# Experts' weights requested as one transfer per matrix in place of two halves

## The reference, cut to what matters

```
xb  = hf[toks]                                   # 128 rows at most, x 1024
hid = silu(xb @ w_g[e]) * (xb @ w_u[e])          # w_g, w_u: 1024 x 512
yb  = (hid @ w_d[e]) * wb[:, None]               # w_d: 512 x 1024
y   = zeros.at[row_tok].add(yb)
```

## Time and profile before

| | us |
|---|---|
| median of 3 runs | 2850.39 (2847.27 to 2853.35) |
| profiled execution, its own time | 2851.61 |
| span of the profiled execution | 2849.8 |
| ACT's first work on experts' weights | 2209.9 |
| second expert's first request | 2231.8 |
| last request of weights issued | 2802.2 |

### The profile page before, as it was taken

The page is one execution under the profiler, slowest core; times in us unless marked ns, Lnnn a source line. Parts: engine busy times, 40 slices in busy tenths (PEclk is TensorE's granted clock), DMA queues, the critical chain, the costliest instruction groups (busy, mean ns, idle before and its releaser), DMA issues.

```text
span 2849.8 us, 36330 instructions
## 1 busy us (share of the span) xinstructions
PE 2702.4 (95%) x13108; PEld 2215.8 (78%) x13118; DVE 1981.0 (70%) x2396; ACT 1467.3 (51%) x2248; POOL 523.4 (18%) x394
## 2 busy tenths in 40 slices
PE   7999999999989999999999989899999899999996
PEld 6787978878767667887888877787778788888875
DVE  6776756565655554565545888898764798989885
ACT  5544436443436665443333457534422577777774
POOL 0000500000117665001000000000010154334332
PEclk9999999999989999999999999999999899999998
DMA  5511057653885764761221100112132799999995
GB/s 173 206 52 59 17 166 279 237 206 109 288 251 128 165 165 126 258 225 37 100 71 48 46 15 1 45 45 82 67 113 111 277 380 376 370 362 367 361 362 171
DMA packets 197118, 492.83 MB, mean 173 GB/s; under 512 B 75089, under 2 KB 75217, under 8 KB 172400
## 3 DMA queue, kind: packets, MB, share of 16 engines
q1 hardware_dynamic: 173760, 448.83, 46.1%
q10 hardware_dynamic: 14000, 25.30, 2.5%
q0 software_dynamic: 9216, 16.81, 2.4%
HBM read 436.01 MB, written 71.63 MB: 178 GB/s over the span
## 4 chain that ended last, share of the span: by engine, by line
PE 53%; DMA 12%; DVE 8%; POOL 6%; issue 4%; ACT 3%; SPq 0%; POOLq 0%; DVEq 0%; ACTq 0%; PEldq 0%
DMA ex_raw<-in_w_up_e 7%; PE ps L1439 7%; PE ps L1442 6%; PE ps L1441 6%; POOL fa_pl L2035 6%; PE ps L921 5%; PE ps L922 5%; PE ps L923 5%; PE ps L3664 4%; DMA ex_raw<-in_w_down_e 3%; DVE ex_w L3814 3%; ACT ex_w L3749 2%; PE ps L3392 1%; PE ps L2767 1%; PE ps L2414 1%
## 5 line engine op out<-in xcount | busy, mean ns | idle before, releaser
L3814 DVE TENSOR_TENSOR ex_w<-ex_raw,ex_w 128x2048 fp32r<-128x2048 f32 x190 | 430.8, 2290 | 63.5 <-ACT ex_w L3749 61.3
L3749 ACT ACTIVATE ex_w<-ex_raw 128x2048 fp32r<-128x2048 f32 x190 | 361.7, 1916 | 107.0 <-DMA ex_raw<-in_w_up_e 59.2
L3664 PE MATMUL ps<-ex_w,ex_xT 128*128 128x512 f32 x1536 | 367.8, 395 | 12.8 <-DVE ex_xT L3829 12.8
L3664 PEld LDWEIGHTS ps<-ex_w,ex_xT 128*128 128x128 f32 x1536 | 287.2, 190 | 78.4 <-issue 13.1
L2035 POOL TENSOR_TENSOR fa_pl<-fa_p,fa_ph 128x512 fp32r<-128x512 f32 x192 | 196.3, 1040 | 108.2 <-ACT fa_ph L2137 104.1
L798 DVE SCALAR_TENSOR_TENSOR arena<-arena,small 128x1023 f32<-128x1023 f32 (+9 forms) x168 | 213.5, 1271 | 3.7
L1571 DVE TENSOR_TENSOR bs_b<-arena,bs_b 128x512 fp32r<-128x512 f32 x160 | 110.4, 690 | 139.4 <-ACT bs_b L1465 139.1
L1465 ACT ACTIVATE bs_b<-arena 128x512 fp32r<-128x512 f32 x160 | 100.1, 629 | 201.6 <-PE ps L1442 178.7
L3664 PE MATMUL ps<-ex_w,ex_hT 128*128 128x512 f32 x768 | 184.5, 396 | 0.7 <-issue 0.5
L3664 PEld LDWEIGHTS ps<-ex_w,ex_hT 128*128 128x128 f32 x768 | 143.0, 189 | 31.3 <-issue 1.9
L1850 DVE TENSOR_REDUCE small<-ps 128x1 f32<-128x512 f32 (+1 forms) x192 | 101.2, 554 | 84.5 <-PE ps L1829 45.4
(11 more groups left out here) (492 smaller groups left out, 6820.5 us busy)
## 6 DMA issues: line engine op xcount, KB each, us to landing
ex_raw<-in_w_gate_e SPq DMA_DIRECT2D x64, 1024.0 KB, 13.8
ex_raw<-in_w_up_e SPq DMA_DIRECT2D x64, 1024.0 KB, 13.6
ex_raw<-in_w_down_e SPq DMA_DIRECT2D x64, 1024.0 KB, 14.1
bs_a<-h_ops SPq DMA_DIRECT2D x100, 512.0 KB, 4.3
arena<-in_w_in SPq DMA_DIRECT2D x56, 512.0 KB, 3.7
zu_a<-h_ops SPq DMA_DIRECT2D x56, 512.0 KB, 3.9
arena<-in_w_in SPq DMA_DIRECT2D x26, 1024.0 KB, 6.5
h_ops<-ko_s SPq DMA_DIRECT2D x16, 512.0 KB, 6.2
```

The lines of the kernel that those rows point to most:

```text
L3664: mm = nc.tensor.matmul(out, l, r, start=(k == 0 and n == 0), stop=(k == kc - 1 and n == 2))
L3749: nc.scalar.activation(half_of(part[m][0], h), raw[m][:, h * W // 2: (h + 1) * W // 2], ACT.Identity).then_inc(high[m], 1)
L3814: V.tensor_tensor(half_of(part[m][1], h), raw[m][:, h * W // 2: (h + 1) * W // 2], half_of(as_f32(part[m][0]), h), ALU.subtract)\
```

## The change

The raw buffers stay as they are. A matrix is now one request of 2 MB with 16 KB per partition, with one semaphore; SP waits until DVE has made both low parts of the previous expert's matrix, and ACT waits for the whole matrix before it begins the first half. ACT's and DVE's instructions stay in halves, and so do PE's waits. The same is done for the last expert's DOWN and for the path that handles experts with more tokens than a place holds.

```
-def load_half(sp, raw, experts, e, loaded, m, h):
-    half = slice(h * KC * DE // 2, (h + 1) * KC * DE // 2)
+def load_whole(sp, raw, experts, e, loaded, m):
     of = experts[m][bass.ds(e, 1)].rearrange("a (p k) n -> p (a k n)", p=P)
-    sp.dma_start(raw[m][:, half], of[:, half]).then_inc(loaded[m][h], 16)
+    sp.dma_start(raw[m], of).then_inc(loaded[m], 16)
...
         def load(i, s, which):
             b = i * ns + s
             for m in which:
-                for h in range(2):
-                    sp.wait_ge(low[m], b * 2 + (h + 1))
-                    load_half(sp, raw, experts, b, loaded, m, h)
+                sp.wait_ge(low[m], b * 2 + 2)
+                load_whole(sp, raw, experts, b, loaded, m)
...
             if now is LAST:
-                for h in range(2):
-                    sp.wait_ge(low[GATE], 2 * NE + 2)
-                    load_half(sp, [raw[GATE]] * 3, experts, NE - 1, [last_loaded] * 3, DOWN, h)
+                sp.wait_ge(low[GATE], 2 * NE + 2)
+                load_whole(sp, [raw[GATE]] * 3, experts, NE - 1, [last_loaded] * 3, DOWN)
...
                 act.wait_ge(used[m], b + 1)
+                act.wait_ge(loaded[m], b * 16 + 16)
                 for h in range(2):
-                    act.wait_ge(loaded[m][h], b * 16 + 16)
                     nc.scalar.activation(half_of(part[m][0], h), raw[m][:, ...
```

More of the change, by code:

```diff
@@ L3467, in expert_raw @@
     return [c.named(f"ex_raw{m}", *((3, 0), (3, W), (5, W))[m], W) for m in range(3)]
-def load_half(sp, raw, experts, e, loaded, m, h):
-    half = slice(h * KC * DE // 2, (h + 1) * KC * DE // 2)
+def load_whole(sp, raw, experts, e, loaded, m):
     of = experts[m][bass.ds(e, 1)].rearrange("a (p k) n -> p (a k n)", p=P)
-    sp.dma_start(raw[m][:, half], of[:, half]).then_inc(loaded[m][h], 16)
+    sp.dma_start(raw[m], of).then_inc(loaded[m], 16)
 def load_expert(sp, raw, experts, e, loaded, which=range(3)):
     for m in which:
-        for h in range(2):
-            load_half(sp, raw, experts, e, loaded, m, h)
+        load_whole(sp, raw, experts, e, loaded, m)
 ExpertPrograms = namedtuple("ExpertPrograms", "sync gpsimd tensor scalar vector half0 half1 stored used")
@@ L3530, in expert_programs @@
     if loaded is None:
-        loaded = [[S(f"loaded{m}{h}") for h in range(2)] for m in range(3)]
+        loaded = [S(f"loaded{m}") for m in range(3)]
     high = [S(f"high{m}") for m in range(3)]
@@ L3536, in expert_programs @@
         gathered = [S("gathered0"), S("gathered1")]
-    last_loaded = [S(f"last_loaded{h}") for h in range(2)]
+    last_loaded = S("last_loaded")
     asked = S("asked")
@@ L3582, in cycle @@
                     for m in range(3):
-                        for h in range(2):
-                            sp.wait_ge(low[(m - 1) % 3], i * 2 + (4 if m else 2))
-                            load_half(sp, raw, experts, no, loaded, m, h)
+                        sp.wait_ge(low[(m - 1) % 3], i * 2 + (4 if m else 2))
+                        load_whole(sp, raw, experts, no, loaded, m)
             run(sp, cycle)
@@ L3755, in hi_last @@
             act.wait_ge(used[GATE], NE + 1)
+            act.wait_ge(last_loaded, 16)
             for h in range(2):
-                act.wait_ge(last_loaded[h], 16)
                 nc.scalar.activation(half_of(last_down[0], h), raw[GATE][:, h * W // 2:(h + 1) * W // 2],
@@ L4319, in _build @@
             raw = expert_raw(c, False)
-            loaded = [[c.sem(ctx, f"ex_loaded{m}{h}") for h in range(2)] for m in range(3)]
+            loaded = [c.sem(ctx, f"ex_loaded{m}") for m in range(3)]
             gathered = [c.sem(ctx, f"ex_gathered{s}") for s in range(2)]
```

## The result

The changed kernel takes 2862.83 us (median of 7 runs, 2856.2 to 2866.38) against 2850.39 of the kernel before (now 7 runs, 2844.37 to 2853.35): ratio 1.0041, 95% interval 1.0026 to 1.0055, so about 12 us slower. On two other chips the same kernel came out at 1.0055 (1.0035 to 1.0075) and 1.0056 (1.0040 to 1.0072). The profiled execution has a span of 2863.2 us against 2849.8, so 13.4 us are to be found.

What follows compares the result with a forecast made beforehand. The DMA engines' work was taken to bound most of the experts' stage. From 2851.61 us, -4.0 (packets), +1.2 (start) and +2.3 (end) gave 2851.1, or 2849.9 carried over to the median; range 2840 to 2860.

Steps and rivals of the forecast that it cites:

- the new wait in the steady part: Experts' stage: ACT waits for whole matrices and requests leave 6.7 us after landing, against 4.3; 1.0 us reserve left, cost nothing.
- the queue that runs empty: Rival, experts' steady part: the reserve of three large requests falls below zero; 0.5 us an expert, +15, 2865; chance 0.05.
- mild form of late splitting: Experts' stage: ACT's first-half split after a late landing delays DVE by only 0.4 us an expert; +12, 2862.
- Term 1: Weights' transfers: 16 KB packets in place of 8 KB save 0.3 us of engine time per MB; -4.0 us over 31 experts.
- Term 2: Start of the experts' stage: SP's first-half request goes out 2.3 us later, waiting for both low parts; +1.2 us.
- Term 3: End of the experts' stage: after the last UP lands both halves are still to be split, one more low part; +2.3 us.
- Late splitting: Rival, experts' stage: DVE stands until ACT makes a first half, waits above 4 us an expert; +30 to +62; chance 0.13.
- Cut in two: Rival, weights' transfers: each 16 KB row still moves as two packets, so no packet saving; 2853.9; chance 0.13.
- Distinctly faster requests: Rival, experts' stage: larger requests cut DMA time by 0.78 us an expert or more, PE sets the pace; 2835.5; chance 0.17.
- The fixed 2.0 us: Weights' requests: a rule gives each request a fixed part beside its bytes, so one fewer saves 2.0 us for each matrix.
- The bound itself: Late experts' stage: the work of the DMA engines, at share 1.00, sets the pace of 18.54 us an expert, against PE's 17.76.

Runs made afterwards that it cites:

- e1: Kernel before, but SP waits for both low parts of each matrix, then requests both 1 MB halves at once; ACT waits as before: 1.0050 of the kernel before.
- e13: The changed kernel once more, with 16 KB packets, run on one chip beside e14: 1.0056 of the kernel before.
- e14: The changed kernel's waits, but with 8 KB packets in 1 MB requests, on the same chip as e13: 1.0051 of the kernel before.
- e3: Kernel before, halves requested one by one, but ACT waits for both halves of a matrix before splitting the first: 1.0013 of the kernel before.
- e4: Kernel before with the tokens' gathered and scattered rows spread over all partitions instead of the low ones: 0.9923 of the kernel before.
- e8: Kernel before with late requests for all three matrices, both halves together, and GATE's another 4 us later: 1.0040 of the kernel before.
- e17: Kernel before, GATE alone late: first half requested after both its low parts, second only after UP's first low part: 1.0011 of the kernel before.
- e18: Kernel before, GATE alone late, both halves requested together when both its low parts are made; same chip as e17: 1.0030 of the kernel before.

## Why the prediction was wrong

- **Failed step: the new wait in the steady part, counted at nothing.** The 6.7 us between landing and request were right, and the landing, foretold at 11.7, came at 12.4, 11.1 and 11.9 for the three matrices. Wrong was the step "The engines stay supplied and the cost is nothing", taken as if the 16 engines were one server that loses time only when the queue is empty. The queue never was: at least three halves were on their way throughout in e1, and e1 costs 0.50%. One matrix asked for in this way costs about 0.1 to 0.3% (DOWN's interval just takes in nothing), and the three add up. Measured in the profile of the changed kernel: 0.33 us an expert over 23 experts, 7.7 us in all, and 3.5 us because transfers took over the pace four experts earlier.
- **The rival that came nearest** is the queue that runs empty, priced at 0.5 us an expert and given 0.05. Its sign, ACT waiting more for landings, is there; its share, which I had said would stay, fell to 0.97, and its mechanism, a reserve below zero, is not what the runs show. The mild form of late splitting names 2862, almost the measured time, but its mechanism isn't there either: that number is luck.
- **Term 1** (-4.0): the engine time per MB fell by about the 0.3 us foretold, and the commonest time of a packet in the traces is 611 ns at 16 KB against 309 at 8 KB, 7 ns less than twice. (The trace of the kernel before does hold 89 packets of 16 KB, all in the instruction queue q8 and of 876 ns and more; the prediction had said that there were none.) No gain in time could be measured (e13 against e14), and the intervals are too wide to exclude one of 4 us.
- **Term 2** (+1.2): 0. **Term 3** (+2.3): right as it was worded, from the landing of the last UP to the end of the span. That is 2849.8 - 2805.0 = 44.8 us before (the row at 2805.04 in the earlier trace rows) and 2863.2 - 2816.2 = 47.0 after, by the row below; but counted from the last GATE request the end grew by 0.6 only, so this landing comes earlier by most of it. ACT's wait alone, e3, costs 4 us over the whole kernel; its profile does not show where.

```profile
2816.21 1.92 ACT ex_w L3744
```

- **Late splitting** (rival): DVE's waits for ACT rose to 2.4 us an expert, not above 4. **Cut in two**: no, 9171 packets. **Distinctly faster requests**: no; the pace of 17.76 is reached by spreading rows (e4), not by larger requests. The fixed 2.0 us of the Trainium skill, DMA: Bandwidth & Descriptors, Anatomy of one DMA, which stood behind this rival, is fitted there to transfers that GpSimd issues, and SP issues these. No run shows 2.0 us saved for each matrix.
- **The bound itself** was named too broadly. A DMA share of 1.00 read as if every engine were needed; spreading the rows over the engines took the wait away.

- **What stood in for it**: not mainly the lateness of the request (e8, e17), but that both halves of a matrix go out together, as shown for GATE (e17 against e18). Holding GATE's first half back until both its buffers are free costs 0.30% if the second goes with it, and 0.11% if the second follows 4 us later.

Open: which engines stand idle and when (the trace does not name the engine of a packet), by what mechanism 2 MB of one matrix at one stroke are worse than 1 MB twice although the queue is never empty, whether that holds for UP and DOWN, and what the 0.11% of e17 are.

## What to carry to other kernels

Where transfers set the pace, give each part of a buffer back as soon as it is free and ask for it at once: halves asked for 2 to 4 us apart beat one request of the same bytes by 0.4 to 0.6%, and fewer, larger packets gave nothing back that could be measured. Before working on requests, look at whether rows of an indirect transfer fill only some of the partitions: spreading them gave 0.7 to 0.8% here, for four small instructions. A reserve worked out as an average over engines and matrices is no cover for a new wait.

## What the runs showed of the hardware that I had not expected

A mean DMA share of 1.00 goes with engines that are not the bound: with the same bytes and packets the landing of 1 MB went from 14.0 to 8.5 us when 64 rows were spread over all partitions, and the share read 1.01. Asking for GATE 4 us later (e8) made its landing 4 us shorter and cost nothing that shows against e1. And two requests of one matrix sent together cost time (0.19% for GATE alone) while no fewer than three halves were on their way.
